# Hybrid decoder layer on one core: pooled channels projected second, VectorE masks its own scores, GpSimd pools and splits the value weights between the projection tiles

## The reference, cut to what matters

```
proj = x @ w_in                # 512 x 1024 times 1024 x 2632: q, k, v, iq, ik, iw, u
score[t,s] = sum_j iw[t,j] * relu(iq[t,j] . ik[s] / 8), -inf where s > t
keep = the 128 best keys s of each query t
A = softmax(q k / 8 + rel_bias[bucket(t - s)], kept keys only) @ v     # 8 heads of 64
u_g = trailing mean of u over 2, 4, 8, 16 positions, minus u           # 4 groups of 128
B = (u_g @ w_pool[g]) * pool_scale
h = LayerNorm(alpha * x + concat(A, B) @ w_out)
h = LayerNorm(alpha * h + HierMoE(h))    # 32 experts, two of one group for each row
```

## Time and profile before

| | us |
|---|---|
| median of 3 runs (lowest, highest) | 571.93 (570.46, 575.38) |
| the profiled execution's own time | 574.13 |
| its span in the profile | 572.4 |
| out of this time ahead of and behind the span | 1.7 |
| TensorE, VectorE, ScalarE, GpSimd busy | 478.4, 228.9, 149.0, 161.7 |

### The profile page before, as it was taken

One profiled execution on the slowest core, in us unless ns is written; L12 is line 12 of the kernel. 1 busy time (PEld: TensorE's weight loads), 2 busy tenths in 40 slices (PEclk: granted clock), 3 DMA queues, 4 the chain that ended last, 5 costly groups with the idle time before them and its releaser, 6 DMA issues.

```text
span 572.4 us, 6202 instructions
## 1 busy us (share of the span) xinstructions
PE 478.4 (84%) x2210; PEld 277.4 (48%) x2210; DVE 228.9 (40%) x562; ACT 149.0 (26%) x313; POOL 161.7 (28%) x158
## 2 busy tenths in 40 slices
PE   4999998999486766999757999899896987778893
PEld 4687775757353435888653433333332333333331
DVE  2101856996688573245580211221111100011197
ACT  3333242532145575032240121111111101111032
POOL 2244331489533593033351022111111001100000
PEclk9999999899798898999856999899798888889897
DMA  9944467204039000993487999999999999999903
GB/s 314 322 51 52 52 176 218 89 1 147 2 141 354 21 0 1 352 409 121 168 346 279 348 408 423 419 420 419 420 420 421 421 422 418 419 422 396 361 28 147
DMA packets 42440, 148.04 MB, mean 259 GB/s; under 512 B 11284, under 2 KB 15892, under 8 KB 30120
## 3 DMA queue, kind: packets, MB, share of 16 engines
q1 hardware_dynamic: 37992, 139.71, 64.7%
q0 software_dynamic: 4320, 7.82, 3.7%
q10 hardware_dynamic: 96, 0.08, 0.0%
HBM read 137.16 MB, written 18.35 MB: 272 GB/s over the span
## 4 chain that ended last, share of the span: by engine, by line
PE 43%; DMA 20%; DVE 16%; SPq 9%; issue 6%; POOL 4%; ACT 2%; DVEq 0%; POOLq 0%; ACTq 0%
PE bank L1316 12%; DMA wgu<-in_w_up_dram 11%; PE bank L1495 9%; PE bank L1435 8%; SPq L496 6%; DMA xe<-h_rows,row_from 5%; PE bank L1519 3%; SPq L499 3%; DVE score L951 2%; DVE m L950 2%; DMA yg<-y_rows 2%; PE bank L1336 2%; DVE score L968 2%; PE bank L1481 2%; PE bank L1363 2%
## 5 line engine op out<-in xcount | busy, mean ns | idle before, releaser
L1495 PE MATMUL bank<-wgu,xeT 128*64 128x512 f32 x512 | 129.6, 665 | 26.6 <-DMA wgu<-in_w_up_dram 25.7
L1495 PEld LDWEIGHTS bank<-wgu,xeT 128*64 128x64 f32 x512 | 43.1, 152 | 102.7 <-issue 101.7
L1142 DVE TENSOR_TENSOR act_row<-bank,sil 128x256 f32<-128x256 f32 x16 | 6.8, 425 | 152.4 <-ACT sil L863 152.4
L716 POOL DMA_INDIRECT y_rows<-ye,row_to x14 | 14.1, 1010 | 177.0 <-PE bank L1481 107.0
L1519 PE MATMUL bank<-wd,actT 128*64 128x512 f32 x256 | 57.9, 593 | 0.7 <-ACT actT L870 0.7
L863 ACT ACTIVATE sil<-bank 128x256 f32<-128x256 f32 x16 | 6.1, 384 | 153.4 <-PE bank L1495 153.4
L618 POOL TENSOR_TENSOR ring_low<-ring,wt_high 128x1024 fp32r<-128x1024 f32 x12 | 28.6, 2387 | 49.1 <-ACT wt_high L743 49.1
L1519 PEld LDWEIGHTS bank<-wd,actT 128*64 128x64 f32 x256 | 19.7, 137 | 35.6 <-issue 35.6
L1316 PE MATMUL bank<-xT_high,ring_low 128*128 128x512 f32 x128 | 32.4, 395 | 0.0
L1363 PE MATMUL bank<-kT,qT 64*128 64x128 f32 (+3 forms) x64 | 15.3, 558 | 17.9 <-DVE nmx L1008 16.9
L681 POOL TENSOR_SCALAR lg<-lg,rinv 128x128 f32<-128x128 f32 (+3 forms) x32 | 19.8, 619 | 35.9 <-DVE rinv L1038 35.9
(11 more groups left out here) (206 smaller groups left out, 748.5 us busy)
## 6 DMA issues: line engine op xcount, KB each, us to landing
wgu<-in_w_gate_dram SPq DMA_DIRECT2D x32, 1024.0 KB, 22.0
wgu<-in_w_up_dram SPq DMA_DIRECT2D x32, 1024.0 KB, 26.8
wd<-in_w_down_dram SPq DMA_DIRECT2D x32, 1024.0 KB, 29.1
ring<-in_w_in_dram SPq DMA_DIRECT2D x5, 2048.0 KB, 14.2
wo<-in_w_out_dram SPq DMA_DIRECT2D x2, 2048.0 KB, 8.1
y_rows<-zero SPq DMA_DIRECT2D x1, 4096.0 KB, 21.7
yg<-y_rows SPq DMA_DIRECT2D x8, 512.0 KB, 9.4
bias_rows<-brow SPq DMA_DIRECT2D x1, 2560.0 KB
```

Of the source, the lines that this page charges most:

```text
L1495: ins = pe.matmul(bank[2 + i][half_rows(n), :], xeT[i][:, k, half_rows(n)], wgu[slots[n]][:, :, k, :], start=k == 0, stop=k == KD - 1)
```

## The change

The order of the groups becomes IQ, U, Q, K, V. Score pairs move to tile 5 (block 1, all eight heads), 8 and 9 (block 2), 12 and 13 (block 3). VectorE masks by adding -1e38 times `tri`, the strict upper triangle, and the two semaphores to GpSimd go. `EARLY_ROUNDS` is 14; the two late rounds stand in units 1 and 2. GpSimd's list is rewritten: a pooling group after the low splits behind tiles 6, 7, 8 and 10, the `bias8` masks behind tile 12, and the low parts of V (`value_low`) behind tiles 13, 14, 15. ScalarE makes `v_high` behind K 0 and K 1. The splits of `wo` rows 4 and 5 move from before the units into units 1, 3 (ScalarE) and 4, 6 (VectorE). SyncE issues wpool and `hfix` right after the ring loads, the other small loads behind the row write, then K, and only then waits for the row write. `ptmp` lies elsewhere, and `wu_high` is gone. TensorE waits for V's high and low parts apart.

```
-        v_sb = at("v_sb", o, [NT, AW])
-        wu_high = [at(f"wu_high{i}", o + 4 * KB * i, [KD, P], F32R) for i in range(2)]
-        o += 8 * KB
+        v_sb = at("v_sb", o, [NT, AW]); o += 8 * KB
...
+        ptmp = [at(f"ptmp{i}", o + 2176 * i, [PAD + SEQ]) for i in range(2)]
...
-        group_cols = [IQ_OFF, Q_OFF, K_OFF, U_OFF, V_OFF]
-        IQ, Q, K, U, V = range(5)
+        group_cols = [IQ_OFF, U_OFF, Q_OFF, K_OFF, V_OFF]
+        IQ, U, Q, K, V = range(5)
         ring_of = [0, 1, 2, 0, 1]
 
-        tiles = [("ik", 0)] + [(g, m) for g in (IQ, Q, K, U, V) for m in range(NA)]
-        units_in = {5: (1, 0, 4), 6: (1, 4, 8), 10: (2, 0, 4), 11: (2, 4, 8), 15: (3, 0, 4), 16: (3, 4, 8)}
+        tiles = [("ik", 0)] + [(g, m) for g in (IQ, U, Q, K, V) for m in range(NA)]
+        units_in = {5: (1, 0, 8), 8: (2, 0, 4), 9: (2, 4, 8), 12: (3, 0, 4), 13: (3, 4, 8)}
...
-            return (ring[ring_of[kind]][:, :, cols], (wu_high if kind == U else wt_high)[i % 2][:, :, :],
+            return (ring[ring_of[kind]][:, :, cols], wt_high[i % 2][:, :, :],
...
-        EARLY_ROUNDS = 4
+        EARLY_ROUNDS = 14
         FIRST_V = tile_no[(V, 0)]
+        pooled_after = [tile_no[(U, 1)], tile_no[(U, 2)], tile_no[(U, 3)], tile_no[(Q, 1)]]
...
-        SMALLS = 8 + NA
+        SMALLS = 8
...
+            sp.dma_start(wpool[:, :, :], w_pool[0].rearrange("g c d -> c g d")).then_inc(small_in, 16)
+            for g in range(NA):
+                sp.dma_start(hfix[:, g, :], headfix[g].partition_broadcast(P)).then_inc(hfix_in, 16)
+            def load_group(g):
+                sp.wait_ge(proj_ps, tile_no[(g - 3, NA - 1)] + 1)
+                sp.dma_start(ring[ring_of[g]][:, :, :], win[:, :, group_cols[g]:group_cols[g] + AW]).then_inc(group_in[ring_of[g]], 16)
             sp.wait_ge(row_ready, 2)
             sp.dma_start(row_dram.ap().rearrange("c h j -> h c j"), brow[0:HEADS, :].unsqueeze(1).to_broadcast([HEADS, P, TW])).then_inc(row_out, 16)
-            sp.wait_ge(row_out, 16)
-            sp.dma_start(bias8[:, :, :], bass.AP(row_dram, P - 1, [[HEADS * TW - 1, P], [TW, HEADS], [1, SEQ]])).then_inc(bias_in, 16)
-            sp.dma_start(wpool[:, :, :], w_pool[0].rearrange("g c d -> c g d")).then_inc(small_in, 16)
             with nc.allow_non_contiguous_dma(reason="2560 elements in all"):
                 sp.dma_start(gT[:, :], ln1_g[0].rearrange("(k p) -> p k", p=P)).then_inc(small_in, 16)
                 sp.dma_start(bT[:, :], ln1_b[0].rearrange("(k p) -> p k", p=P)).then_inc(small_in, 16)
                 sp.dma_start(pscale[:, :], pool_scale[0].rearrange("(g p) -> p g", p=P)).then_inc(small_in, 16)
-            for g in range(NA):
-                sp.dma_start(hfix[:, g, :], headfix[g].partition_broadcast(P)).then_inc(small_in, 16)
             sp.dma_start(wr[:, :, 0:GROUPS], w_r1[0].rearrange("(k p) n -> p k n", p=P)).then_inc(small_in, 16)
             sp.dma_start(wr[:, :, GROUPS:], w_r2[0].rearrange("(k p) n -> p k n", p=P)).then_inc(small_in, 16)
             sp.dma_start(br[:, 0:GROUPS], b_r1[0].partition_broadcast(P)).then_inc(small_in, 16)
             sp.dma_start(br[:, GROUPS:], b_r2[0].partition_broadcast(P)).then_inc(small_in, 16)
-            for g in range(3, 5):
-                sp.wait_ge(proj_ps, tile_no[(g - 3, NA - 1)] + 1)
-                sp.dma_start(ring[ring_of[g]][:, :, :], win[:, :, group_cols[g]:group_cols[g] + AW]).then_inc(group_in[ring_of[g]], 16)
+            load_group(K)
+            sp.wait_ge(row_out, 16)
+            sp.dma_start(bias8[:, :, :], bass.AP(row_dram, P - 1, [[HEADS * TW - 1, P], [TW, HEADS], [1, SEQ]])).then_inc(bias_in, 16)
+            load_group(V)
             wov = w_out[0].rearrange("(k p) n -> p k n", p=P)
-            sp.wait_ge(proj_ps, tile_no[(U, NA - 1)] + 1)
+            sp.wait_ge(proj_ps, tile_no[(K, NA - 1)] + 1)
             sp.dma_start(wo[1][:, :, :], wov[:, KD // 2:KD, :]).then_inc(wo_in[1], 16)
...
-                    pool.wait_ge(small_in, 16 * SMALLS)
+                    pool.wait_ge(hfix_in, 16 * NA)
...
-            for item in front:
-                if item[0] == "tile":
-                    tile_low(item[1] + 2)
-                    g = item[1] - tile_no[(U, 1)]
-                    if 0 <= g < NA - 1:
-                        mix_group(g)
-                elif item[0] == "score" and item[2] == HEADS - 1:
-                    b = item[1]
-                    pool.wait_ge(score_sum, b)
-                    d = score[:, P * b:P * b + P]
-                    pool.affine_select(out=d, in_=d, compare_op=ALU.is_ge, fill=NONCAUSAL, base=0, pattern=[[-1, P]],
-                                       channel_multiplier=1).then_inc(score_masked, 1)
-                    if b == NT - 1:
-                        pool.wait_ge(bias_in, 16)
-                        for hh in range(HEADS):
-                            pool.affine_select(out=bias8[:, hh, :], in_=bias8[:, hh, :], compare_op=ALU.is_ge, fill=-BIG, base=SEQ - P,
-                                               pattern=[[-1, SEQ]], channel_multiplier=1).then_inc(bias_ready, 1)
-            mix_group(NA - 1)
+            def value_low(c):
+                pool.wait_ge(v_high_ready, c + 1)
+                pool.tensor_tensor(ring_low[ring_of[V]][:, 2 * c:2 * c + 2, :], ring[ring_of[V]][:, 2 * c:2 * c + 2, :],
+                                   v_high[:, 2 * c:2 * c + 2, :].bitcast(F32), ALU.subtract).then_inc(v_low_ready, 1)
+            for i in range(LATE):
+                tile_low(i + 2)
+                if i in pooled_after:
+                    mix_group(pooled_after.index(i))
+                if i == tile_no[(Q, NA - 1)]:
+                    pool.wait_ge(bias_in, 16)
+                    for hh in range(HEADS):
+                        pool.affine_select(out=bias8[:, hh, :], in_=bias8[:, hh, :], compare_op=ALU.is_ge, fill=-BIG, base=SEQ - P,
+                                           pattern=[[-1, SEQ]], channel_multiplier=1).then_inc(bias_ready, 1)
+                for c in {tile_no[(K, 0)]: (0,), tile_no[(K, 1)]: (1, 2), tile_no[(K, 2)]: (3,)}.get(i, ()):
+                    value_low(c)
...
-                    if (kind, m) == (V, 1):
-                        act.wait_ge(wo_in[1], 16)
-                        act.wait_ge(row_out, 16)
-                        for k in range(KD // 2, KD - 2):
-                            act.activation(wo_high[k][:, :], wo[1][:, k - KD // 2, :], ACT.Copy).then_inc(wo_high_ready, 1)
-                    if (kind, m) == (K, NA - 1):
+                    if kind == K and m < 2:
                         act.wait_ge(group_in[ring_of[V]], 32)
-                        for c in range(4):
+                        for c in (2 * m, 2 * m + 1):
                             act.activation(v_high[:, 2 * c:2 * c + 2, :], ring[ring_of[V]][:, 2 * c:2 * c + 2, :], ACT.Copy).then_inc(v_high_ready, 1)
...
-                if u in (9, 11):
-                    k = KD - 2 + (u - 9) // 2
+                if u in (1, 3, 9, 11):
+                    k = KD // 2 + (1, 3, 9, 11).index(u)
+                    if u == 1:
+                        act.wait_ge(wo_in[1], 16)
+                        act.wait_ge(row_out, 16)
                     act.activation(wo_high[k][:, :], wo[1][:, k - KD // 2, :], ACT.Copy).then_inc(wo_high_ready, 1)
...
+            dve.wait_ge(consts_ready, 2)
...
-                dve.sem_inc(score_sum, 1)
-                dve.wait_ge(score_masked, b)
+                d = score[:, P * b:P * b + P]
+                link(dve.scalar_tensor_tensor(out=d, in0=tri[:, :], scalar=NONCAUSAL, in1=d, op0=ALU.mult, op1=ALU.add))
                 for r in range(TOPK // 8 if b < NT - 1 else EARLY_ROUNDS):
                     topk_round(b)
                 if b < NT - 1:
                     mark_kept(b)
-                if b == 2:
-                    for c in range(4):
-                        dve.wait_ge(v_high_ready, c + 1)
-                        dve.tensor_tensor(ring_low[ring_of[V]][:, 2 * c:2 * c + 2, :], ring[ring_of[V]][:, 2 * c:2 * c + 2, :],
-                                          v_high[:, 2 * c:2 * c + 2, :].bitcast(F32), ALU.subtract).then_inc(v_low_ready, 1)
...
-            for k in range(KD // 2, KD - 2):
-                wo_second_half_low(k)
...
-                if u < late_rounds:
+                if 1 <= u <= late_rounds:
                     topk_round(NT - 1)
-                elif u == late_rounds:
+                elif u == late_rounds + 1:
                     mark_kept(NT - 1)
...
-                if u in (14, 15):
-                    wo_second_half_low(KD - 2 + u - 14)
+                if u in (4, 6, 14, 15):
+                    wo_second_half_low(KD // 2 + (4, 6, 14, 15).index(u))
...
-                    if (kind, m) == (V, 0):
-                        pe.wait_ge(v_low_ready, 4)
-                    elif kind != V:
+                    if kind != V:
                         pe.wait_ge(wt_high_ready, i + 1)
+                    elif m == 0:
```

(8 more changed lines are left out.)

4 lines of the change are left out of this document (1 added, 3 removed).

## The result

The changed kernel takes 553.23 us (median of 4 runs, 552.97 to 554.10), the kernel before 573.65 beside it: ratio 0.9651, 95% interval 0.9597 to 0.9706. Forecast was 555, range 548 to 563; its gain was 17.1 us, the measured one is 20.4 by these medians. The profiled execution took 552.97 us with a span of 551.2, 21.2 shorter than before.

A forecast was written before the change was run, and what follows sets the result against it. The unit loop started on GpSimd's word (pooling), some 9 us after TensorE was ready. Gains of 14.7 (units 0 to 7) and 2.4 (units 8 to 15) gave 571.9 - 17.1 = 554.8, said as 555 us; range 548 to 563.

The forecast's parts named there:

- rivals 2 and 5: Respectively: K weights landing at 122, kernel slower, 578 us (0.03); expert stream giving back attention's gain, 571 us (0.05).
- TensorE's tiles: Projection on TensorE: reordered tiles run without a stop, first logits at 136.4 instead of 141.10 us.
- The second way to the sum: Projection end on TensorE: the time before, less the stop (2.75) and the slow matmuls (2.07), gives 135.6 us.
- K weights: Load for projection tile 13: issued from 46 us at the earliest, landing at 88, needed by 99, no stop.
- The upper bound of 100: Latest K landing: nothing through until the row write ends, 15.7 us of small loads, 9.3 to land; stop of 1 us.
- Rival 1: Projection: K weights land between 99 and 110, TensorE stops at tile 13, total 560 us; chance 0.12.
- VectorE's selection: Score sums, masks and MAX8 rounds before the loop: 14 rounds of block 3 end at 130, 6 us before the logits.
- GpSimd: Pooling between weight splits, ready 30 us earlier; value splits end at 125.1, 3 us before TensorE wants them at 128.3.
- Rival 3: GpSimd or its port late: pooling and splits slow each other, V 0 waits 3 to 5 us, total 559; chance 0.08.
- Units 0 to 7: First loop stage: 14.2 us, TensorE next to bound it; unit 8's logits at 150.6 instead of 165.31, gain 14.7 us.
- Units 8 to 15: Second loop stage: rounds leave VectorE, busiest engine at ratio 0.70; gain 2.4 us, bounds 0 to 7.
- Rival 4: Loop relaxes fully: units 8 to 15 fall to ScalarE's 11.6 us, total 550; chance 0.12.

The follow-up runs named there:

- a_k_first: Changed kernel with the K load issued right behind the row write, ahead of the small loads: 554.78 us (1 run).
- a_k_behind: Changed kernel with the K load issued behind the wait for the row write and behind the bias load: 555.03 us, ratio 0.9647 to the kernel before.
- a_pool_last: Changed kernel with all four pooling groups behind the value splits on GpSimd's list: 565.66 us, ratio 0.9873 to the kernel before.
- a_vlow_dve: Changed kernel with the four low parts of V back on VectorE: 561.60 us, ratio 0.9792 to the kernel before.
- a_mask_pool: Changed kernel with the three masks of the score blocks back on GpSimd: 555.65 us, ratio 0.9690 to the kernel before.
- a_early12: Changed kernel with 12 early rounds in place of 14: 555.12 us, ratio 0.9668 to the kernel before.
- the two c_: Changed kernel with VectorE's low splits of wo rows and attention mix one unit later, 547.26 us; the same with VectorE's reciprocal also moved ahead, 546.40 us.
- c_dve_later: Changed kernel with VectorE's low splits of wo rows and of the attention mix one unit later: 547.26 us, ratio 0.9528 to the kernel before.

## Why the prediction was right, step by step

**The bound, and where the gain would arise: right.** The start of the units hung on GpSimd. It is shown from both sides: with pooling last the changed kernel loses 12.4 of its 20 us, and neither early rounds nor an early load gives the kernel before its first unit below 149. What the forecast took from unit 8's start, 14.7 us, came as 14.8; the stages behind it became no longer, so it arrived whole and rivals 2 and 5 fell. The total is less exact than it looks: the gain was forecast as 17.1 us and is 21.2 by the profiled executions, and 555 lies within 2 us of 553.23 because it was counted from a median of 571.93, 1.7 below the 573.65 measured beside the change. Of the signs named, VectorE's first unit was to start at 136 to 138, released by TensorE's logits, and 14 rounds to end near 130: neither came.

**TensorE's tiles: right.** 135.93 for 136.4, no stop, value pass at 127.74 for 128.3. The half microsecond is block 1's four pairs in a row. The second way to the sum mixes row lengths with starts: from the starts, 95.92 to 105.98 for 5.44, stop and slow matmuls cost 4.62 and not 4.82, which changes nothing.

**K weights: right by a path that was wrong in part.** Landing at 87.0 for 88, but not because the early issue got through: SyncE was held for 53 us, and K went out at 78.34. The upper bound of 100 allowed 15.7 us for the small loads once the row write was done; in fact the three slow ones had been issued by 76.0, stalled beside it and not after it, and the other four took 2.3. The sentence that the early issue brings nothing before the row write's end is too strong as well: a_k_first got half of K in. And a_k_behind shows that the order of K and bias load decides nothing. Rival 1 fell.

**VectorE's selection: the step that failed.** Rounds that were to end at 130 ended at 138.8. Its parts: block 1 right (57.26 for 57.2); block 2's rounds 20.0 us for 20.1, block 3's 21.3 for 21.3. All of the 8.8 us lies in sums and masks: the first MAX8 of block 2 is 4.4 late, that of block 3 another 4.6 (9.0 against the 129.8 of the unrounded sum). The prediction let the sums keep pace with TensorE's pairs and the mask cost 0.2 to 0.5; it priced GpSimd's slowdown beside VectorE but not VectorE's beside GpSimd, and said that groups 0 and 2 fall on rounds, where group 2 fell on block 2's sums (78 to 85). The price could be read from the kernel before: two 384-wide sums took 1.27 us beside an idle GpSimd, and its seven 512-wide sums 8.85 beside the first pooling groups. a_pool_last gives back 5.4 of it, and a_vlow_dve 2.1 in one mask. What is left is at least in part the same: with pooling last block 3's seven sums still take 981 ns each beside the eight bias masks, and in a_mask_pool, where GpSimd stands idle from 110.4 to 113.9, the median of those that run then is 752. The rule quoted from the Trainium skill (SBUF — State Buffer, Who interferes with whom), two SBUF inputs on VectorE against a reading GpSimd, holds in both directions here: 0.29 became 1.27 and 2.38, while MAX8 rounds kept their length.

It did no harm by luck: the cover was not where the prediction had it. It named 6 us before the logits; those were overspent by 2.9. What covered was what the prediction had counted as TensorE's work in units 0 to 7: the twelve value matmuls between first and second logits, 3.4 us. a_early12 and a_vlow_dve bracket it: 3 us earlier brings nothing, 4.6 later costs 4.6.

**GpSimd: right, by less.** Value splits at 126.84 for 125.1, cover 0.9 for 3. They kept 2.37 each beside MAX8 (7.12 for three). The bias masks stretched, 6.23 for 4.59, but ended at 110.2, and GpSimd then stood idle 1.73 us for ScalarE's half of the next weights. ScalarE's timeline names the cause:

```profile
106.73 0.60 ACT L775 ACTIVATE relu<-bank 128x512 f32<-128x512 f32 x1 [5.21 <-DVE score L959]
...
110.75 1.06 ACT L738 ACTIVATE wt_high<-ring 128x1024 fp32r<-128x1024 f32 x1
```

ScalarE waited 5.21 us until VectorE, late with block 2, freed a buffer of `relu`, and its split stood behind that. So VectorE's lateness did reach the tightest hand-off, over a path that the prediction doesn't have, and the 1.73 us are most of what is missing from the 3 us of cover. a_mask_pool ends the value splits 1.3 us later against the tiles, and TensorE waits. Rival 3 fell by 0.9 us.

**Units 0 to 7: right.** 14.56 for 14.2, TensorE busy for 14.42 of it at full clock, which is the bound named.

**Units 8 to 15: right direction, mis-sized.** The gain was 4.1 for 2.4, inside its bounds of 0 to 7. The same 14.54 or 14.55 stands in every other kernel that has no rounds there, but for the two c_, so it is what the stage takes without rounds. The busiest engine fills 0.76 of it, not 0.70. Rival 4's 11.6 was not reached: TensorE still stops 1.16, 0.29 and 2.82 us for VectorE's maxima before units 12, 14 and 16. What holds VectorE there was not tested; c_dve_later takes only 0.3 us out of the stage.

**From unit 16 on: nothing, as said.** 1.1 us less, at a lower clock. That nothing was to be had from the change here was right; c_dve_later shows that the stage itself still held 6.4 us.

## What to carry to other kernels

Before a unit loop, list for each engine when it is truly ready, and look which one gives the word: freeing another (here by an earlier load) mostly lengthens its wait, 8.46 us for 4.78. When work moves between VectorE and GpSimd, price both sides of the pair, and by the operation of VectorE that will run beside it: its two-input sums took 1.6 to 2.1 times and its masks 4 to 8 times their length beside an idle GpSimd, its MAX8 rounds no longer than before. Then follow a late engine through those that wait for it: VectorE's lateness reached GpSimd by way of ScalarE. And where two engines each hold half of a split, put the second half one unit later: the exchange of waits between them was worth 6 us, about half of what moving the pooling was.
